# Decoder step on one core: the causal mask of the stick-breaking logits moves from a TensorE product to a GpSimd select

## The chip, the cores and the metric

One NeuronCore of a Trainium2 chip runs the whole program. The metric is the device time of one execution in microseconds (us); where several executions are shown, their median counts. Engines are named as in the profile: PE is TensorE (PEld its weight loads), DVE VectorE, ACT ScalarE, POOL GpSimd, SP the queue that issues the transfers. S, Z, O, TR, OU and three G are the eight PSUM banks.

## The reference, cut to what matters

One layer of a decoder: input projections of 520 token columns (512 prompt tokens and 8 decoding ones), three token mixers, a gated merge, an output projection and an MLP. The change touches the stick-breaking attention of the prompt, 8 heads by 4 blocks of 128 queries. Its logits are strictly causal, a key counts for a query only if it stands before it:

```python
def sb_block(q, k, v, q_pos, k_pos, b_sb):
    z = (jnp.einsum('bqhd,bkhd->bhqk', q, k).astype(jnp.float32) * (HEAD_DIM ** -0.5)
         + b_sb.astype(jnp.float32)[None, :, None, None])
    valid = k_pos[None, :] < q_pos[:, None]
    log_keep = jnp.where(valid, jax.nn.log_sigmoid(-z), 0.0)
    after = lax.cumsum(log_keep, axis=3, reverse=True) - log_keep
    a = jnp.where(valid, jnp.exp(jax.nn.log_sigmoid(z) + after), 0.0)
    return jnp.einsum('bhqk,bkhd->bqhd', a.astype(v.dtype), v)
```

Where a logit is -1e30, both the log of what is kept and the weight come out as 0, so that the mask can be written into the logits.

## The kernel before, in words

All weights are split into a high and a low part so that PE can work with full precision: `split_hi` on ACT (L675, 128x1024) copies the raw tile into whi, `split_lo` (on POOL for nearly all units, L638) subtracts it and writes wlo. A unit is one 128-wide weight tile; a tick is one half (260 columns) of one unit: 24 products G<-xh,whi / xl,whi / xh,wlo in `project` (L1277), in two parts. The result goes to one of three G banks, from which ACT takes it (`take`, L703).

The rest of the kernel is hung between these ticks. `make_plan` (L180) gives every stage a tick; each engine walks through all ticks in order and issues its share of the stages behind its own work of that tick. The order is fixed when the program is written, and each engine works strictly in it.

The 36 steps of the stick-breaking attention, `PSEQ` (L172), are 32 prompt steps "p" (block i of queries, head h, with 128*(i+1) keys) and 4 decoding steps "d". Step m starts at tick 20+m:

- tick 20+m: PE forms the logits in bank S (`p_scores`, L1343): a product of skT and sqT (64 rows, fp32, two records in the profile), and onto its last 128 columns a second, bf16 product of an identity and a strictly upper mask of -1e30 (identb, maskb).
- tick 21+m: ACT (`p_weights`, L779) scales bank S into pz (L786), which frees the bank, then runs Abs, Exp and Ln over it (psp, L796 to L798); DVE (`p_weights`, L1121) makes psp, a scan into pw, and pw minus pz.
- tick 23+m: ACT takes Exp of pw (`p_exp`, L800) at the tick's start; PE turns pw into bank TR (`p_turn`, L1352) at its end; DVE copies it to pT (L1133).
- tick 24+m: PE forms the weighted sum (`p_sum`, L1360) in bank OU.

At every odd tick of this stretch ACT issues a `split_hi` between its take and its `p_weights`, and POOL answers with a `split_lo` of some 2.4 us. POOL has nothing else to do there but one memset. The masks are made once at the program's start:

```python
            nc.gpsimd.affine_select(out=maskb[:], in_=maskb[:], compare_op=ALU.is_gt, fill=MASK, base=0,
                                    pattern=[[-1, P]], channel_multiplier=1).then_inc(consts_made, 1)
```

The chain of one step crosses the engines like this in ACT's part:

```python
                    nc.scalar.activation(z, src[:, keys], ACT.Identity, scale=SCALE,
                                         bias=bsb[:, h:h + 1]).then_inc(of(read, "p_scores", n), 1)
                    await_taken(act, "p_scores", n)
```

Of the kernel before, what the change touches and what calls it, by code (L numbers as in the profile page):

```python
# [10 lines left out]
BF16 = mybir.dt.bfloat16  # L11
I32 = mybir.dt.int32
ALU = mybir.AluOpType
# [3 lines left out]
P = 128  # L17
# [7 lines left out]
SBH = 8  # L25
# [7 lines left out]
MASK = -1e30  # L33
# [77 lines left out]
def at(kind, tile, half=1):  # L111
    return AT[kind, tile, half]
# [59 lines left out]
PSEQ = []  # L172
# [126 lines left out]
def decoder_step(nc, x, o):  # L299

    ctx = ExitStack()
    with ctx:
        def sem(name):
            return ctx.enter_context(nc.semaphore(name))
# [4 lines left out]
        base = 16512  # L309

        def place(name, shape, col, dt=F32):
            return nc.alloc_sbuf_tensor_at(name, shape, dt, offset=base + 4 * col)
# [4 lines left out]
        whi = place("whi", [P, 2, KC, P], 11392, F32R)  # L317
        wlo = place("wlo", [P, 2, KC, P], 13440, F32R)
        ident = place("ident", [P, P], 15488)
        identb = place("identb", [P, P], 15616, BF16)  # L320
        maskb = place("maskb", [P, P], 15680, BF16)
        ones = place("ones", [P, P], 15744)
        cvec = place("cvec", [P, NCV], 15872)
        c0 = 15872 + (NCV + 7) // 8 * 8
# [30 lines left out]
        sqT = place("sqT", [P, 4, TOK], R)  # L355
        skT = place("skT", [P, 4, TOK], R + 2080)
        svT = place("svT", [P, 4, TOK], R + 4160)
        sv_tok = place("sv_tok", [P, QB, 512], R + 7280)
        pz = place("pz", [P, 2, 512], R + 9360)
# [65 lines left out]
        written = {n: sem(f"written_{n}") for n in ("S", "TR", "OU")}  # L425
        read = {n: sem(f"read_{n}") for n in ("S", "TR", "OU", "Z", "O")}
        act_done, dve_done, pool_done = sem("act_done"), sem("dve_done"), sem("pool_done")
        consts_made = sem("consts_made")
# [3 lines left out]
        kv_in = [sem(f"kv_in{i}") for i in range(KVS)]  # L432
        kv_used = sem("kv_used")
        qz_zero, qd_zero_made, qz_made, qd_made = sem("qz_zero"), sem("qd_zero_made"), sem("qz_made"), sem("qd_made")
        p_lnmade, p_wmade, p_amade = sem("p_lnmade"), sem("p_wmade"), sem("p_amade")
        bias_in_slot = [sem(f"bias_in_slot{i}") for i in range(2)]
        l_made, l_pmade = sem("l_made"), sem("l_pmade")
        sk_out, sv_out, dk_out, dv_out, conv_out, conv_copy = (
# [16 lines left out]
        def raw(u):  # L455

            if u < U_MLP:
                return wraw[:, u % WR], w_in_slot[u % WR], 16 * (u // WR + 1)
            m = u - U_MLP
            return mraw[:, m % MR], m_in_slot[m % MR], 16 * (m // MR + 1)  # L460

        def high(u):
            return mhigh[:, u - U_END] if u >= U_END else whi[:, u % 2]

        def low(u):
            return mlow[:, (u - U_MLP) % MR] if u >= U_END else wlo[:, u % 2]
# [12 lines left out]
        def open_bank(pe, *key):  # L479
            name, n = SPOT[key]  # L480
            if n:
                pe.wait_ge(read[name], n)
            return bank[name]

        def await_bank(eng, *key):
            name, n = SPOT[key]
            eng.wait_ge(written[name], n + 1)
            return bank[name]

        def await_taken(eng, *key):  # L490
            name, n = SPOT[key]
            eng.wait_ge(read[name], n + 1)

        def of(sems, *key):
            return sems[SPOT[key][0]]
# [10 lines left out]
        def head(h):  # L506
            return h // 2, slice(HD * (h % 2), HD * (h % 2) + HD)
# [114 lines left out]
        @block.gpsimd  # L622
        def _(pool):
            nc.gpsimd.memset(ones[:], 1.0).then_inc(consts_made, 1)
            nc.gpsimd.memset(ident[:], 0.0).then_inc(pool_done, 1)
            nc.gpsimd.memset(identb[:], 0.0).then_inc(pool_done, 1)
            nc.gpsimd.memset(maskb[:], 0.0).then_inc(pool_done, 1)
            nc.gpsimd.memset(qz[:], 0.0).then_inc(qz_zero, 1)
            nc.gpsimd.memset(Q192[:], 0.0).then_inc(qz_zero, 1)
            nc.gpsimd.memset(wT[:, PAGES * 64:], 0.0).then_inc(qz_zero, 1)  # L630
            pool.wait_ge(pool_done, 3)
            for m in (ident, identb):
                nc.gpsimd.affine_select(out=m[:], in_=m[:], compare_op=ALU.not_equal, fill=1.0, base=0,
                                        pattern=[[-1, P]], channel_multiplier=1).then_inc(consts_made, 1)
            nc.gpsimd.affine_select(out=maskb[:], in_=maskb[:], compare_op=ALU.is_gt, fill=MASK, base=0,
                                    pattern=[[-1, P]], channel_multiplier=1).then_inc(consts_made, 1)

            def split_lo(u):  # L638
                pool.wait_ge(w_hi, u + 1)
                nc.gpsimd.tensor_tensor(low(u), raw(u)[0], high(u).bitcast(F32), ALU.subtract).then_inc(w_lo, 1)  # L640

            split_lo(0)
            for kc in range(1, KC, 2):
                pool.wait_ge(rstd0_made, 2)
                if kc >= 3:
                    pool.wait_ge(xl_made, kc - 1)
                nc.gpsimd.tensor_tensor(xn[:, 1, :], xraw[:, kc, :], rstd0[:], ALU.mult).then_inc(xn_pool, 1)
            split_lo(1)

            def qd_zero(_):  # L650
                pool.wait_ge(xl_made, KC)
                nc.gpsimd.memset(qd[:], 0.0).then_inc(qd_zero_made, 1)

            stages = dict(qd_zero=qd_zero)
            for k, (u, job, h, last) in enumerate(TICKS):
                for v in SPLIT_AFTER.get(k, []):
                    if not LO[v][0]:
                        split_lo(v)
                for stage, n in PLAN[2 * k] + PLAN[2 * k + 1]:
                    if stage in stages:  # L660
                        stages[stage](n)

        @block.scalar
        def _(act):
            done = [0]

            def link(ins):
                done[0] += 1
                ins.then_inc(act_done, 1)
                act.wait_ge(act_done, done[0])  # L670
# [108 lines left out]
            def p_weights(m):  # L779
                what, n = PSEQ[m]  # L780
                if what == "p":
                    i, h = n // SBH, n % SBH
                    keys = slice(0, P * (i + 1))
                    src = await_bank(act, "p_scores", n)
                    z, l = pz[:, m % 2, keys], psp[:, m % 2, keys]
                    nc.scalar.activation(z, src[:, keys], ACT.Identity, scale=SCALE,  # L786
                                         bias=bsb[:, h:h + 1]).then_inc(of(read, "p_scores", n), 1)
                    await_taken(act, "p_scores", n)
                else:
                    act.wait_ge(kv_used, 8 * (n + 1))  # L790
                    src = bank[SPOT["d", n][0]]
                    z, l = pz[:, m % 2, :], psp[:, m % 2, :]
                    nc.scalar.activation(z, src[:, :], ACT.Identity, scale=SCALE,
                                         bias=bcol).then_inc(of(read, "d", n), 1)
                    await_taken(act, "d", n)
                link(nc.scalar.activation(l, z, ACT.Abs))  # L796
                link(nc.scalar.activation(l, l, ACT.Exp, scale=-1.0))
                nc.scalar.activation(l, l, ACT.Ln, bias=1.0).then_inc(p_lnmade, 1)  # L798
# [78 lines left out]
            def h_ready_tile(t):  # L877
                act.wait_ge(dve_took, EVAC[at("out", t)][1])
                if t:
# [5 lines left out]
            stages = dict(qz=qz_fill, qd=qd_fill, sv_rows=sv_rows, dv_rows=dv_rows, dvs=dvs_fill, p_weights=p_weights,  # L885
                          p_exp=p_exp, p_turn=p_turn, p_sum=p_sum, v_red=v_red, l_weights=l_weights,
                          l_turn=l_turn, l_out=l_out, s_soft=s_soft, s_turn=s_turn, s_red=s_red,
                          branch_split=branch_split)
# [375 lines left out]
        def _(pe):  # L1264
            def mm(out, lhsT, rhs, start, stop, **kw):
                return nc.tensor.matmul(out, lhsT, rhs, start=start, stop=stop, **kw)  # L1266
# [1 line left out]
            def turn(out, in_, rows=P):  # L1268
                return nc.tensor.transpose(out, in_, ident[0:rows, 0:rows])  # L1269

            pe.wait_ge(consts_made, 4)
            pe.wait_ge(xacc_made, KC)
            for h in range(2):
                dst = open_bank(pe, "x_var", h)
# [68 lines left out]
            def p_scores(n):  # L1343
                i, (t, rows) = n // SBH, head(n % SBH)
                keys = P * (i + 1)
                if n == 0:
                    pe.wait_ge(act_took, EVAC[at("sk", 3)][1])
                dst = open_bank(pe, "p_scores", n)
                mm(dst[:, 0:keys], sqT[rows, t, P * i:P * i + P], skT[rows, t, 0:keys], True, False)
                mm(dst[:, keys - P:keys], identb[:], maskb[:], False, True).then_inc(of(written, "p_scores", n), 1)  # L1350

            def p_turn(m):  # L1352
                what, n = PSEQ[m]
# [143 lines left out]
            def l_out(t):  # L1497
# [4 lines left out]
            stages = dict(sv_rows=sv_rows, dv_rows=dv_rows, dk=dk, p_scores=p_scores, p_turn=p_turn, p_sum=p_sum,  # L1502
                          v_sum=v_sum, v_red=v_red, s_k=s_k, s_self=s_self, s_turn=s_turn, s_v=s_v,
                          s_vself=s_vself, s_red=s_red, l_scores=l_scores, l_turn=l_turn, l_sum=l_sum, l_out=l_out)
# [160 lines left out]
```

## Time and profile before

| | before |
|---|---|
| median of 3 executions | 1193.66 us (1190.55 to 1194.98) |
| the profiled execution, its own time | 1195.64 us |
| its span | 1193.9 us |
| mean granted clock of PE | 0.982 of full speed |
| busy: PE, PEld, DVE, ACT, POOL | 94%, 83%, 34%, 37%, 27% |
| the stick-breaking steps of the prompt | ticks 20 to 60, from 106 to 349 us |

A row of the order in time reads: start in us, duration in us, engine, source line, operation, what is written and read, shape, how many are merged, and in brackets how long the engine was idle before it and who ended that. "MATMUL S<-maskb,identb" is the mask product, "pz<-S" the copy out of bank S, "TR<-ident,pw" the turn of the weights.

### The profile page before, as it was taken

The numbers are of one execution on the slowest core, as the hardware profiler recorded it, in microseconds if no ns is written. First come the engines' busy times: TensorE is split into PE (matmuls) and PEld (weight loads), VectorE is DVE, ScalarE is ACT, GpSimd is POOL, SyncE is SP. The second block draws the span as 40 slices with busy tenths as digits, with TensorE's granted clock in tenths as the row PEclk, the third lists the DMA queues.
The fourth block names the chain that finished last, engine by engine and source line by source line (L and its number), as shares of the span: only waits on it lengthen the run. The fifth ranks groups of instructions, "written<-read, shape, count | busy, mean of one in ns | idle before, by whom it ended". The sixth has DMA issues, their size and how long they took to land.

```text
span 1193.9 us, 21778 instructions
## 1 busy us (share of the span) xinstructions
PE 1119.1 (94%) x8650; PEld 994.3 (83%) x8650; DVE 406.0 (34%) x680; ACT 442.0 (37%) x796; POOL 318.0 (27%) x146
## 2 busy tenths in 40 slices
PE   2998899999999999999999999998999999999995
PEld 1886666667776767667899999998999999999995
DVE  6101233443432244241204344675312312222444
ACT  5223354555442322324332232345413413413544
POOL 3432122211112111100121212123444444444540
PEclk9999899999999999999999999998999999999998
DMA  7369666655468645544124223472765674665402
GB/s 234 124 196 307 223 204 195 184 209 181 142 210 295 193 156 185 150 151 147 54 89 161 89 97 98 159 295 78 270 218 180 238 263 172 236 244 206 159 1 72
DMA packets 65847, 210.91 MB, mean 177 GB/s; under 512 B 7850, under 2 KB 10059, under 8 KB 63571
## 3 DMA queue, kind: packets, MB, share of 16 engines
q1 hardware_dynamic: 65746, 209.52, 52.3%
q8 instruction: 69, 1.13, 0.4%
q14 instruction: 32, 0.25, 0.1%
HBM read 202.02 MB, written 51.48 MB: 212 GB/s over the span
## 4 chain that ended last, share of the span: by engine, by line
PE 86%; ACT 5%; DVE 4%; issue 2%; DMA 1%; SPq 0%; POOL 0%; DVEq 0%; ACTq 0%; POOLq 0%
PE G L1266 54%; PE S L1266 10%; PE Z L1266 9%; PE O L1266 8%; PE OU L1266 3%; PE TR L1269 2%; ACT whi L673 2%; DVE convy L960 1%; ACT pz L786 1%; DVE xl L960 1%; DMA wraw<-in_w_in_dram 1%; DMA xraw<-in_xt_dram 0%; PE TR L1266 0%; DVE mtmp L960 0%; DVE macc L957 0%
## 5 line engine op out<-in xcount | busy, mean ns | idle before, releaser
L1266 PE MATMUL G<-xh,whi 128*128 128x260 f32 x1312 | 389.5, 297 | 13.5 <-DVE xl L960 11.8
L1266 PE MATMUL G<-xl,whi 128*128 128x260 f32 x1312 | 376.6, 287 | 0.0
L1266 PE MATMUL G<-xh,wlo 128*128 128x260 f32 x1312 | 376.1, 287 | 0.0
L640 POOL TENSOR_TENSOR wlo<-wraw,whi 128x1024 fp32r<-128x1024 f32 x63 | 153.4, 2435 | 618.4 <-ACT whi L673 618.4
L1266 PEld LDWEIGHTS G<-xh,whi 128*128 128x128 f32 x1312 | 253.0, 193 | 52.6 <-issue 37.9
L1266 PEld LDWEIGHTS G<-xl,whi 128*128 128x128 f32 x1312 | 253.6, 193 | 0.0
L1266 PEld LDWEIGHTS G<-xh,wlo 128*128 128x128 f32 x1312 | 253.4, 193 | 0.0
L640 POOL TENSOR_TENSOR wlo<-mraw,whi 128x1024 fp32r<-128x1024 f32 x56 | 134.9, 2409 | 200.6 <-ACT whi L673 200.5
L673 ACT ACTIVATE whi<-wraw 128x1024 fp32r<-128x1024 f32 x84 | 88.4, 1053 | 85.6 <-PE G L1266 77.2
L673 ACT ACTIVATE whi<-mraw 128x1024 fp32r<-128x1024 f32 x56 | 59.4, 1061 | 157.0 <-PE G L1266 54.6
L960 DVE SCALAR_TENSOR_TENSOR psp<-pz,psp 128x512 f32<-128x512 f32 (+3 forms) x36 | 24.6, 684 | 142.2 <-ACT psp L798 142.2
L960 DVE SCALAR_TENSOR_TENSOR lg<-S,bias 128x256 f32<-128x256 f32 (+3 forms) x48 | 22.0, 457 | 105.2 <-PE S L1266 105.2
L731 ACT ACTIVATE tg<-G,cvec 128x260 f32<-128x260 f32 x48 | 22.9, 477 | 88.7 <-PE G L1266 88.7
L957 DVE TENSOR_TENSOR wlo<-wraw,whi 128x1024 fp32r<-128x1024 f32 x21 | 25.7, 1224 | 86.6 <-ACT whi L673 86.6
L673 ACT ACTIVATE lT<-TR 128x256 f32<-128x256 f32 (+3 forms) x48 | 19.6, 409 | 94.4 <-PE TR L1269 94.4
L1266 PE MATMUL G<-hidl,whi 128*128 128x260 f32 x192 | 54.4, 283 | 0.0
L1266 PE MATMUL G<-hidh,whi 128*128 128x260 f32 x192 | 54.3, 283 | 0.0
L1266 PE MATMUL G<-hidh,wlo 128*128 128x260 f32 x192 | 54.1, 282 | 0.0
L957 DVE TENSOR_TENSOR hidl<-msq,hidh 128x260 fp32r<-128x260 f32 x64 | 45.6, 714 | 4.8 <-ACT hidh L673 4.8
L1266 PE MATMUL G<-binh,whi 128*128 128x260 f32 x160 | 45.5, 284 | 1.6 <-issue 1.6
L1266 PEld LDWEIGHTS OU<-dv_tok,lT 128*128 128x128 f32 x216 | 28.0, 190 | 22.1 <-issue 17.4
L957 DVE TENSOR_TENSOR hT<-hT,G 128x260 f32<-128x260 f32 x47 | 19.9, 423 | 77.0 <-PE G L1266 77.0
(270 smaller groups left out, 2246.1 us busy)
## 6 DMA issues: line engine op xcount, KB each, us to landing
wraw<-in_w_in_dram SPq DMA_DIRECT2D x66, 512.0 KB, 4.8
kv<-in_kpool_dram SPq DMA_DIRECT2D x128, 256.0 KB, 3.2
kv<-in_vpool_dram SPq DMA_DIRECT2D x128, 256.0 KB, 3.1
mraw<-in_w_up_dram SPq DMA_DIRECT2D x32, 512.0 KB, 3.4
mraw<-in_w_down_dram SPq DMA_DIRECT2D x32, 512.0 KB, 3.4
out_win_k_kept_dram<-in_cache_win_k_dram SPq DMA_DIRECT2D x8, 2047.0 KB, 9.5
out_win_v_kept_dram<-in_cache_win_v_dram SPq DMA_DIRECT2D x8, 2047.0 KB, 10.8
wraw<-in_w_ab_dram SPq DMA_DIRECT2D x8, 512.0 KB, 3.3
```

The lines of the kernel that those rows point to most:

```text
L640: nc.gpsimd.tensor_tensor(low(u), raw(u)[0], high(u).bitcast(F32), ALU.subtract).then_inc(w_lo, 1)
L673: return nc.scalar.activation(out, in_, ACT.Copy, **kw)
L731: nc.scalar.activation(tg[tile % 4][:, g, half(h)], src, ACT.Tanh, scale=0.5, bias=bgate[:, g, tile:tile + 1]).then_inc(act_took, 1)
L786: nc.scalar.activation(z, src[:, keys], ACT.Identity, scale=SCALE, bias=bsb[:, h:h + 1]).then_inc(of(read, "p_scores", n), 1)
L957: return nc.vector.tensor_tensor(out, a, b, op)
L960: return nc.vector.scalar_tensor_tensor(out, a, scalar, b, op0, op1)
L1266: return nc.tensor.matmul(out, lhsT, rhs, start=start, stop=stop, **kw)
L1269: return nc.tensor.transpose(out, in_, ident[0:rows, 0:rows])
```

## The change

The mask is no longer added by PE. POOL writes it: behind ACT's copy of the logits into pz, a select on POOL fills the part on and above the diagonal of pz's last 128 columns with -1e30, in place, and counts the new semaphore `p_masked`. ACT, which read pz back at once, now waits for `p_masked` before Abs. The 32 mask products and the two bf16 constants with their memsets and selects go away, and PE's first wait is for two constants in place of four.

```diff
@@ the constants on POOL
-            nc.gpsimd.memset(identb[:], 0.0).then_inc(pool_done, 1)
-            nc.gpsimd.memset(maskb[:], 0.0).then_inc(pool_done, 1)
...
-            pool.wait_ge(pool_done, 3)
-            for m in (ident, identb):
-                nc.gpsimd.affine_select(out=m[:], in_=m[:], compare_op=ALU.not_equal, fill=1.0, base=0,
-                                        pattern=[[-1, P]], channel_multiplier=1).then_inc(consts_made, 1)
-            nc.gpsimd.affine_select(out=maskb[:], in_=maskb[:], compare_op=ALU.is_gt, fill=MASK, base=0,
+            pool.wait_ge(pool_done, 1)
+            nc.gpsimd.affine_select(out=ident[:], in_=ident[:], compare_op=ALU.not_equal, fill=1.0, base=0,
                                     pattern=[[-1, P]], channel_multiplier=1).then_inc(consts_made, 1)
@@ a new stage on POOL
-            stages = dict(qd_zero=qd_zero)
+            def p_weights(m):
+                what, n = PSEQ[m]
+                if what == "p":
+                    i = n // SBH
+                    await_taken(pool, "p_scores", n)
+                    own = pz[:, m % 2, P * i:P * i + P]
+                    nc.gpsimd.affine_select(out=own, in_=own, compare_op=ALU.is_gt, fill=MASK, base=0,
+                                            pattern=[[-1, P]], channel_multiplier=1).then_inc(p_masked, 1)
+
+            stages = dict(qd_zero=qd_zero, p_weights=p_weights)
@@ p_weights on ACT
-                    await_taken(act, "p_scores", n)
+                    act.wait_ge(p_masked, n + 1)
@@ the start of PE
-            pe.wait_ge(consts_made, 4)
+            pe.wait_ge(consts_made, 2)
@@ p_scores on PE
-                mm(dst[:, 0:keys], sqT[rows, t, P * i:P * i + P], skT[rows, t, 0:keys], True, False)
-                mm(dst[:, keys - P:keys], identb[:], maskb[:], False, True).then_inc(of(written, "p_scores", n), 1)
+                mm(dst[:, 0:keys], sqT[rows, t, P * i:P * i + P], skT[rows, t, 0:keys], True,
+                   True).then_inc(of(written, "p_scores", n), 1)
```

POOL's order before, from the last load of the start-up to the end of the weight splits that read wraw; wlo is the low part of a weight tile and waits for ACT's high part (w_hi):

```order
L640 TENSOR_TENSOR wlo<-wraw,whi 128x1024 [waits w_hi] x19
L652 MEMSET qd 128x1536 [waits xl_made]
L640 TENSOR_TENSOR wlo<-wraw,whi 128x1024 [waits w_hi] x43
```

POOL's order now, the first part of the same stretch:

```order
L633 TENSOR_TENSOR wlo<-wraw,whi 128x1024 [waits w_hi] x12
L653 AFFINE_SELECT pz<-pz 128x128 [waits read_S]
L633 TENSOR_TENSOR wlo<-wraw,whi 128x1024 [waits w_hi]
L653 AFFINE_SELECT pz<-pz 128x128 [waits read_S] x2
L633 TENSOR_TENSOR wlo<-wraw,whi 128x1024 [waits w_hi]
L653 AFFINE_SELECT pz<-pz 128x128 [waits read_S] x2
L633 TENSOR_TENSOR wlo<-wraw,whi 128x1024 [waits w_hi]
L653 AFFINE_SELECT pz<-pz 128x128 [waits read_S]
L633 TENSOR_TENSOR wlo<-wraw,whi 128x1024 [waits w_hi]
```

The selects stand one or two to a gap between the splits: the select of an odd tick comes directly behind that tick's split, the one of an even tick has no split ahead of it.

ACT's order around tick 27, before (whi is the high part of the tile that POOL's split reads):

```order
L673 ACTIVATE dqT<-G 128x260 [waits made]
L673 ACTIVATE whi<-wraw 128x1024 [waits made,w_in_slot0]
L786 ACTIVATE pz<-S,cvec 128x128 [waits written_S]
L796 ACTIVATE psp<-pz 128x128 [waits read_S]
L797 ACTIVATE psp<-psp 128x128 [waits act_done]
L798 ACTIVATE psp<-psp 128x128 [waits act_done]
L804 ACTIVATE pw<-pw 128x128 [waits p_wmade]
```

And now:

```order
L675 ACTIVATE dqT<-G 128x260 [waits made]
L675 ACTIVATE whi<-wraw 128x1024 [waits made,w_in_slot0]
L788 ACTIVATE pz<-S,cvec 128x128 [waits written_S]
L798 ACTIVATE psp<-pz 128x128 [waits p_masked]
L799 ACTIVATE psp<-psp 128x128 [waits act_done]
L800 ACTIVATE psp<-psp 128x128 [waits act_done]
L806 ACTIVATE pw<-pw 128x128 [waits p_wmade]
```

Nothing moved on ACT; one instruction waits for POOL instead of for ACT itself, and the Exp of pw, which belongs to an earlier step, stands behind it.

## Rows read from the trace of the kernel before

**Rows 1.** The page: the span and PE's busy time.

```profile
span 1193.9 us, 21778 instructions
PE 1119.1 (94%) x8650; PEld 994.3 (83%) x8650; DVE 406.0 (34%) x680; ACT 442.0 (37%) x796; POOL 318.0 (27%) x146
```

**Rows 2.** The page: the chain that ended last, by engine.

```profile
PE 86%; ACT 5%; DVE 4%; issue 2%; DMA 1%; SPq 0%; POOL 0%; DVEq 0%; ACTq 0%; POOLq 0%
```

**Rows 3.** Waits of PE, 104 to 350 us: in total, times, longest (us).

```profile
PE S L1266 <- ACT pz L786: 19.0, 17, 4.5
```

**Rows 4.** Order in time, PE: a prompt step with 256 keys, mask product included.

```profile
171.22 0.70 PE L1266 MATMUL S<-skT,sqT 64*128 64x256 f32 x2 [1.68 <-ACT pz L786]
...
171.85 0.23 PE L1266 MATMUL S<-maskb,identb 128*128 128x128 bf16 x1
...
172.09 0.28 PE L1266 MATMUL G<-xl,whi 128*128 128x260 f32 x1
```

**Rows 5.** Order in time, PE: logits of the other attention, same shape, no mask.

```profile
386.27 0.70 PE L1266 MATMUL S<-dkT,dqT 64*128 64x256 f32 x2
...
386.90 0.39 PE L1266 MATMUL G<-xh,whi 128*128 128x260 f32 x1
...
387.12 0.28 PE L1266 MATMUL G<-xl,whi 128*128 128x260 f32 x1
```

**Rows 6.** Groups by form on POOL: busy us, mean ns of one, idle before.

```profile
L640 POOL TENSOR_TENSOR wlo<-wraw,whi 128x1024 fp32r<-128x1024 f32 x63 | 153.4, 2435 | 618.4 <-ACT whi L673 618.4
L633 POOL TENSOR_SCALAR_AFFINE_SELECT ident<-ident 128x128 f32<-128x128 f32 x1 | 0.3, 292 | 0.0
```

**Rows 7.** Order in time, ticks 27 and 28.

```profile
151.63 2.39 POOL L640 TENSOR_TENSOR wlo<-wraw,whi 128x1024 fp32r<-128x1024 f32 x1 [10.23 <-ACT whi L673]
...
151.84 0.31 ACT L796 ACTIVATE psp<-pz 128x128 f32<-128x128 f32 x1
...
152.75 0.29 ACT L804 ACTIVATE pw<-pw 128x128 f32<-128x128 f32 x1
...
152.87 1.30 DVE L960 SCALAR_TENSOR_TENSOR psp<-pz,psp 128x128 f32<-128x128 f32 x1 [1.74 <-ACT psp L798]
...
153.97 0.33 PE L1269 MATMUL TR<-ident,pw 128*128 128x128 f32 x1
```

**Rows 8.** Order in time, ticks 37 and 38.

```profile
209.32 2.40 POOL L640 TENSOR_TENSOR wlo<-wraw,whi 128x1024 fp32r<-128x1024 f32 x1 [8.37 <-ACT whi L673]
...
209.63 0.42 ACT L796 ACTIVATE psp<-pz 128x256 f32<-128x256 f32 x1
...
210.85 0.40 ACT L804 ACTIVATE pw<-pw 128x256 f32<-128x256 f32 x1
...
212.20 0.44 PE L1269 MATMUL TR<-ident,pw 128*128 128x128 f32 x2
```

**Rows 9.** Order in time, ticks 47 and 48.

```profile
269.95 2.41 POOL L640 TENSOR_TENSOR wlo<-wraw,whi 128x1024 fp32r<-128x1024 f32 x1 [10.57 <-ACT whi L673]
...
270.38 0.53 ACT L796 ACTIVATE psp<-pz 128x384 f32<-128x384 f32 x1
...
273.46 0.52 ACT L804 ACTIVATE pw<-pw 128x384 f32<-128x384 f32 x1
...
274.04 0.55 PE L1269 MATMUL TR<-ident,pw 128*128 128x128 f32 x3 [0.58 <-ACT pw L804]
```

**Rows 10.** Order in time, ticks 39 and 40.

```profile
221.39 0.61 ACT L804 ACTIVATE pw<-pw 128x512 f32<-128x512 f32 x1
...
224.70 0.66 PE L1269 MATMUL TR<-ident,pw 128*128 128x128 f32 x4
```

**Rows 11.** Stretches behind waits: us, busy by engine (instructions), granted clock, DMA share, GB/s.

```profile
171.00:177.00 6.00, 5.78 (x43) 3.73 (x43) 2.11 (x3) 1.62 (x5) 2.26 (x1) 1.00 0.42 148
184.00:190.00 6.00, 6.00 (x35) 4.71 (x39) 1.60 (x3) 2.17 (x6) 1.49 (x1) 0.72 0.63 192
...
582.00:588.00 6.00, 6.00 (x38) 6.00 (x39) 0.00 (x0) 0.66 (x2) 0.00 (x0) 0.72 0.29 87
```

More of the change, by code:

```diff
@@ L319, in decoder_step @@
         ident = place("ident", [P, P], 15488)
-        identb = place("identb", [P, P], 15616, BF16)
-        maskb = place("maskb", [P, P], 15680, BF16)
         ones = place("ones", [P, P], 15744)
@@ L434, in decoder_step @@
         qz_zero, qd_zero_made, qz_made, qd_made = sem("qz_zero"), sem("qd_zero_made"), sem("qz_made"), sem("qd_made")
-        p_lnmade, p_wmade, p_amade = sem("p_lnmade"), sem("p_wmade"), sem("p_amade")
+        p_lnmade, p_wmade, p_amade, p_masked = sem("p_lnmade"), sem("p_wmade"), sem("p_amade"), sem("p_masked")
         bias_in_slot = [sem(f"bias_in_slot{i}") for i in range(2)]
```

## The prediction, made before the changed kernel ran

> **What bounds the kernel now.** I read the page first: PE works 94% of the span [rows 1], and of the chain that ended last 86% lie on it [rows 2]. So only what lengthens or shortens PE's own row moves the end. Then the waits of PE in the stretch of the change: it idles there nearly only for bank S, freed by ACT's copy into pz, 17 times and 19.0 us in all, 4.5 us of them in one wait [rows 3]. All three engines that the change touches meet in that stretch, and what must be seen is the order in time around each step.
>
> **What the change takes from PE.** The mask product shows 0.23 us [rows 4], and 32 of them would be 7.4 us. But matmuls are pipelined, so I compare what a step costs with and without it. With 256 keys and the mask, the second G product begins 172.09 - 171.22 = 0.87 us after the logits' start [rows 4]. The other attention forms logits of the same shape with no mask, and there it is 387.12 - 386.27 = 0.85 us [rows 5]. The mask runs in the bubble that the change from S to G leaves anyway. It gives back 0.02 us, and 32 times that is **0.6 us**.
>
> A rule speaks for a larger gain. The Trainium skill, TensorE: Matmul & The Clock Gate, section "Back-to-back issue gap", gives about 81 ns for a sustained pair of weight load and product with 128 columns. By it 32 products would be 2.6 us and the sum below 6.4 us instead of 8.4. The trace's pair of steps disagrees, and I go by it.
>
> **What the change adds on POOL.** A select of 128x128 fp32 took 0.292 us at the start of the program; a weight split takes 2.435 us for 1024 columns [rows 6], which is 0.30 us for 128, so the two agree. That is the value I take; bounds are below. 32 selects are 9.3 us on an engine that is busy 27% [rows 1], free in itself. What counts is where they stand. ACT now copies, waits for POOL, then goes on to Abs, Exp, Ln and, behind them, to the Exp of pw for which PE's next turn waits.
>
> *Even ticks* (15 steps "p"): POOL is idle. ACT stands still for 0.29 us and two hand-overs. A hand-over between engines takes 0.06 us where the rows show one at its limit: pw ends at 273.98 and PE's turn starts at 274.04 [rows 9]. About 0.4 us each, and ACT is busy only 37% [rows 1]: nothing of it reaches PE.
>
> *Odd ticks* (17 steps "p"): `split_hi` stands right before the copy on ACT, and so POOL has just begun the split of 2.4 us when the copy is done. The select waits for all of it. In tick 27 POOL's split ends at 151.63 + 2.39 = 154.02, the select at 154.31, ACT can go on at about 154.38 instead of 151.84 [rows 7]. That is a **delay of 2.5 us**, and of 2.4 to 2.5 us in ticks 37 and 47 [rows 8, 9]. It is paid where PE's turn (TR<-ident,pw) of the next tick stands less than that behind the end of pw's Exp:
>
> - tick 28: pw ends at 152.75 + 0.29 = 153.04 and PE turns at 153.97, 0.93 us later [rows 7]. 2.54 - 0.93 and 0.06 to hand over: **1.7 us** of new wait.
> - tick 38: split ends 211.72, select 212.01, Abs 212.08 instead of 209.63, delay 2.45; pw ended 211.25, the turn stood at 212.20, 0.95 later [rows 8]: **1.5 us**, 1.6 with the hand-over.
> - tick 48: PE already waits 0.58 us for pw there, so there is no cover. Split ends 272.36, Abs 272.72 instead of 270.38 [rows 9]: **2.3 us** on top, a wait of 2.9 us.
>
> In both of the first two PE has no decoding product between its G products, so the tick is short. I put each of the other odd ticks to the same test: the narrowest is tick 40, where pw ends at 222.00 and the turn stands at 224.70, 2.7 us of cover against 2.5 [rows 10]. ACT's next take is up to 2 us late after some of them, but its G bank is wanted three ticks later. The splits themselves do not get later: POOL's next one waits for ACT two ticks on. Together **5.6 us**.
>
> *DVE* is not late by all of that. Its psp<-pz,psp of 128 columns lasted 1.30 us in tick 27 and ended at 154.17, right behind POOL's split at 154.02 [rows 7]: it stood still while POOL worked. The Trainium skill, SBUF — State Buffer, section "Who interferes with whom", says that a DVE instruction with two SBUF inputs and a GpSimd one that reads SBUF lock each other out for a whole instruction; the trace agrees. In the changed kernel DVE starts after the select and is no longer held, so its chain is late by about 1.5 us, not 2.5, and pw of that step is needed more than a tick later. Nothing for PE.
>
> *The start*: PE waits for DVE there, not for the constants. Nothing. No transfer is moved; those that wait for PE come later by as much as PE does.
>
> **What the waits do to PE's clock.** Behind some waits the granted clock falls from 2.4 to 1.2 GHz for a while: the 6 us from 184 on, behind such a wait, show 0.72, while behind the wait of 1.68 us that ends at 171.22 [rows 4] they show 1.00 [rows 11]. A fall costs 6 x 0.28 = 1.7 us. From the wait at 171.22 to the stretch at 582, I find nine waits of over 1.1 us, and five had a fall behind them; first and last of those stretches, and one more, stand in [rows 11]. The two longest of the nine both had one, of the seven from 1.1 to 1.7 us three. For new waits of 1.7, 1.6 and 2.9 us that makes 0.43 + 0.43 + 1, about two falls: **3.4 us**.
>
> **The sum.** 5.6 - 0.6 + 3.4 = **8.4 us**. Against the profiled execution's own 1195.64 that is 1204.0; it stood 2.0 above the median of 1193.66, and against that the forecast is **1202.0 us**, slower by 0.7%. What can be told from no change is about 0.5%, 6 us.
>
> **The rivals.**
>
> *The clock doesn't follow* (no new fall, or one that takes an old one's place, or some of the three waits better covered than here). Then it is 5.6 - 0.6 = 5.0, 1198.7 us, not to be told from no change. For it: four of the seven waits of this size had no fall. Against it: the one of 2.9 us.
>
> *The select is dearer on pz than on the constant.* Only one size and one place was seen; a far bound is a whole microsecond, below half a split [rows 6]. Then 0.7 us more at each of three places is 2.1, tick 40 is short of cover by 0.5, and its like (cover of 2.7 to 3 us) by a few tenths each: some 3.6 in all, 1205.7 us. For it: the agreement with the split's price per column says nothing of a fixed part in another state. Against it: 0.292 includes the fixed part.
>
> *PE gets the whole product back* (the other side). If removing it freed 0.23 us each time, in place of 0.02, PE would gain 7.4 and lose 5.6: 1191.9 us, and with two falls 1195.3, in either case no longer slower. It decides from 5.6 / 32 = 0.175 us a product. Against it stands the pair of steps [rows 4, 5], 0.87 and 0.85 us; for it only that the two steps follow different work.
>
> That the select doesn't do what it should, I see no way for: ACT's own wait for it comes ahead of every reader of pz.
>
> **How the numbers follow.** Forecast, three waits and one to three falls (6.7 to 10.1): 0.58. Clock doesn't follow: 0.27. Dearer select: 0.10. Whole product back, or the three places covered: 0.05. The bound of 6 us lies just under the case of one fall, so 0.62 for slower by over 0.5%, taken from the forecast's case and the dearer select with a little off; 0.34 within 0.5%; 0.04 faster. The range goes from 1196.5, half of the waits and no fall, to 1207.0, three falls and a select of twice the price; it leaves out some 0.15.
>
> **What would show it right or wrong.** In the profile after: PE's waits in the turn (TR<-ident,pw) for pw, 0.6 us before in one wait [rows 9], should be about 6 us in three, the longest 2.9 and in tick 48; a new wait of ACT's psp for POOL's pz of some 2.4 us at 17 steps and 0.4 at 15, 47 us in all or a little less; psp<-pz,psp on DVE without the long cases; bank S steps of 0.85 us; 32 selects of 0.29 us. If the turn's waits make less than 3 us, my cover is wrong; if they are there and the time isn't, it is the clock; if the step without mask is far below 0.85, it is the price of the product.

## The result and the profile after

The changed kernel takes 1205.06 us in the median of six executions (1200.87 to 1209.96), against 1193.79 us of the kernel before: a ratio of 1.010, with a 95% interval of 1.0072 to 1.0128. Six more executions in a later comparison gave 1204.75 us and 1.008 (1.0054 to 1.0106). The forecast was 1202.0 us with a range of 1196.5 to 1207.0, so the change makes the kernel slower, as forecast, and by some more than forecast. Times of kernels are medians of executions, and each kernel is compared with executions of the kernel before that ran beside it.

The page of the changed kernel, its span and busy time; its own time is 1203.70 us, 8.1 more than that of the profiled execution before:

```profile
span 1201.9 us, 21772 instructions
...
PE 1121.4 (93%) x8618; PEld 995.2 (83%) x8618; DVE 399.9 (33%) x680; ACT 441.0 (37%) x796; POOL 325.9 (27%) x174
```

PE is busy 2.3 us longer than before [rows 1] although 32 products are gone; its products run longer where the clock is lower. The rest of the 8.0 us by which the span grew, 5.7 us, is idle time of PE. The chain by engine is nearly what it was [rows 2], with POOL at 1% where it had 0%:

```profile
PE 86%; ACT 5%; DVE 4%; issue 3%; DMA 1%; POOL 1%; SPq 1%; DVEq 0%; ACTq 0%; POOLq 0%
```

The waits of PE from 104 to 360 us; the numbers are the total, how many and the longest, in us:

```profile
PE S L1268 <- ACT pz L788: 19.1, 17, 4.6
PE TR L1271 <- ACT pw L806: 5.7, 3, 2.8
```

The waits for bank S are as long as before [rows 3]. New is the wait of PE's turn for ACT's pw: three waits and 5.7 us, where before there was one of 0.6 us. They stand in ticks 28, 38 and 48 and last 1.51, 1.38 and 2.83 us. What ACT waits for in the same stretch:

```profile
ACT psp L798 <- POOL pz L653: 45.4, 32, 2.5
```

At 17 odd ticks it waits 1.9 to 2.5 us, at 15 even ones mostly 0.47. The select itself, as a group (busy us, mean ns, idle before), takes 307 ns in the mean, against 292 on a constant [rows 6]:

```profile
L653 POOL TENSOR_SCALAR_AFFINE_SELECT pz<-pz 128x128 f32<-128x128 f32 x32 | 9.8, 307 | 61.0 <-ACT pz L788 61.0
```

Ticks 27 and 28 of the changed kernel in order of time, the answer to [rows 7]:

```profile
148.93 2.39 POOL L633 TENSOR_TENSOR wlo<-wraw,whi 128x1024 fp32r<-128x1024 f32 x1 [6.69 <-ACT whi L675]
...
151.27 0.29 POOL L653 TENSOR_SCALAR_AFFINE_SELECT pz<-pz 128x128 f32<-128x128 f32 x1
151.60 0.31 ACT L798 ACTIVATE psp<-pz 128x128 f32<-128x128 f32 x1 [2.50 <-POOL pz L653]
...
152.50 0.29 ACT L806 ACTIVATE pw<-pw 128x128 f32<-128x128 f32 x1
152.62 0.29 DVE L962 SCALAR_TENSOR_TENSOR psp<-pz,psp 128x128 f32<-128x128 f32 x1 [4.20 <-ACT psp L800]
...
152.84 0.33 PE L1271 MATMUL TR<-ident,pw 128*128 128x128 f32 x1 [1.51 <-ACT pw L806]
```

The split runs from 148.93 to 151.32, the select directly behind it. ACT goes on at 151.60 after standing still for 2.50 us, the Exp of pw ends at 152.79, and PE turns 0.05 us later, having waited 1.51. Ticks 37 and 38, the answer to [rows 8]:

```profile
209.62 2.38 POOL L633 TENSOR_TENSOR wlo<-wraw,whi 128x1024 fp32r<-128x1024 f32 x1 [6.72 <-ACT whi L675]
...
212.28 0.42 ACT L798 ACTIVATE psp<-pz 128x256 f32<-128x256 f32 x1 [2.38 <-POOL pz L653]
...
213.95 0.44 PE L1271 MATMUL TR<-ident,pw 128*128 128x128 f32 x2 [1.38 <-ACT pw L806]
```

Ticks 47 and 48, the answer to [rows 9]:

```profile
273.15 2.40 POOL L633 TENSOR_TENSOR wlo<-wraw,whi 128x1024 fp32r<-128x1024 f32 x1 [6.95 <-ACT whi L675]
...
275.50 0.29 POOL L653 TENSOR_SCALAR_AFFINE_SELECT pz<-pz 128x128 f32<-128x128 f32 x1
275.83 0.52 ACT L798 ACTIVATE psp<-pz 128x384 f32<-128x384 f32 x1 [2.29 <-POOL pz L653]
...
278.91 0.52 ACT L806 ACTIVATE pw<-pw 128x384 f32<-128x384 f32 x1
...
279.48 0.55 PE L1271 MATMUL TR<-ident,pw 128*128 128x128 f32 x3 [2.83 <-ACT pw L806]
```

Here the wait grew from 0.58 to 2.83 us, by 2.25. The clock behind the three waits (stretch, its length, busy by engine, granted clock, DMA share, GB/s):

```profile
153.00:159.00 6.00, 6.00 (x38) 5.05 (x40) 3.69 (x7) 3.52 (x8) 0.00 (x0) 0.72 0.78 244
214.00:220.00 6.00, 6.00 (x32) 2.94 (x32) 4.33 (x8) 2.95 (x6) 0.00 (x0) 0.72 0.30 112
280.00:286.00 6.00, 6.00 (x33) 4.82 (x33) 3.38 (x5) 2.58 (x5) 0.00 (x0) 0.72 0.01 2
```

All three show 0.72 as the mean granted clock: in each the clock fell from 2.4 to 1.2 GHz for a while. A step with 256 keys, for [rows 4, 5]:

```profile
171.58 0.70 PE L1268 MATMUL S<-skT,sqT 64*128 64x256 f32 x2 [1.68 <-ACT pz L788]
...
172.20 0.39 PE L1268 MATMUL G<-xh,whi 128*128 128x260 f32 x1
...
172.43 0.29 PE L1268 MATMUL G<-xl,whi 128*128 128x260 f32 x1
```

From the logits to the second G product it takes 172.43 - 171.58 = 0.85 us, what the maskless step of the other attention took [rows 5], and 0.02 less than with the mask [rows 4].

**The time split in two.** Each execution comes with its span and its mean granted clock. Span times (1 - clock) is the time that the clock withheld; the remainder is an estimate of what the span would be at full clock, good as far as PE sets the pace. Every execution's time is 1.7 to 1.9 us longer than its span. The clock is given to three decimals, which fixes one execution's split to 0.6 us only, so I use means over executions. The ratio is to the kernel before in the same comparison:

| kernel | executions | median us | ratio to before (95%) | withheld us | remainder us |
|---|---|---|---|---|---|
| before, all | 73 | 1195.15 | 1 | 20.2 | 1173.2 |
| changed, all | 12 | 1204.76 | 1.010 and 1.008 | 25.5 | 1177.5 |
| select first, all ticks | 12 | 1193.68 | 0.9983 (0.9968 to 0.9998) | 17.9 | 1173.6 |
| select first, three ticks | 12 | 1193.84 | 0.9991 (0.9977 to 1.0005) | 19.3 | 1172.8 |
| before, no mask product | 12 | 1194.84 | 0.9998 (0.9981 to 1.0015) | 19.6 | 1172.9 |
| changed, waits filled | 10 | 1200.55 | 1.0053 (1.0032 to 1.0074) | 21.6 | 1177.7 |
| before, wait only | 6 | 1206.11 | 1.0095 (1.0062 to 1.0127) | 27.5 | 1177.5 |
| changed, select twice | 4 | 1207.24 | 1.0097 (1.0066 to 1.0128) | 27.4 | 1177.9 |
| before, copy first | 6 | 1183.13 | 0.9892 (0.9865 to 0.9918) | 17.1 | 1164.0 |
| select first, copy first | 6 | 1185.71 | 0.9909 (0.9882 to 0.9935) | 19.1 | 1164.3 |

The change costs 1177.5 - 1173.2 = 4.3 us of remainder and 25.5 - 20.2 = 5.3 us withheld. With the spread of the executions (95%) the first is known to 0.9 us and the second to 2.0.

### The profile page after: what moved, and what is told of

Same layout as the page of the kernel before. It is cut to its first block, busy times and chain, and to the rows that moved or that the text cites. A ratio compares the mean times of both kernels' runs of the same rounds, so it can differ in the third digit from the quotient of the medians.

```text
span 1201.9 us, 21772 instructions
## 1 busy us (share of the span) xinstructions
PE 1121.4 (93%) x8618; PEld 995.2 (83%) x8618; DVE 399.9 (33%) x680; ACT 441.0 (37%) x796; POOL 325.9 (27%) x174
## 4 chain that ended last, share of the span: by engine, by line
PE 86%; ACT 5%; DVE 4%; issue 3%; DMA 1%; POOL 1%; SPq 1%; DVEq 0%; ACTq 0%; POOLq 0%
PE G L1268 54%; PE S L1268 10%; PE Z L1268 8%; PE O L1268 8%; PE OU L1268 3%; PE TR L1271 2%; ACT whi L675 2%; DVE convy L962 1%; ACT pz L788 1%; DVE xl L962 1%; DMA wraw<-in_w_in_dram 0%; PE TR L1268 0%; DMA xraw<-in_xt_dram 0%; DVE mtmp L962 0%; DVE macc L959 0%
## 5 line engine op out<-in xcount | busy, mean ns | idle before, releaser
L962 DVE SCALAR_TENSOR_TENSOR psp<-pz,psp 128x512 f32<-128x512 f32 (+3 forms) x36 | 18.5, 513 | 177.3 <-ACT psp L800 177.3
L675 ACT ACTIVATE lT<-TR 128x256 f32<-128x256 f32 (+3 forms) x48 | 19.6, 409 | 97.3 <-PE TR L1271 97.3
L1268 PE MATMUL G<-binh,whi 128*128 128x260 f32 x160 | 45.4, 284 | 1.6 <-issue 1.6
```

What stands on the lines that cost most here:

```text
L675: return nc.scalar.activation(out, in_, ACT.Copy, **kw)
L962: return nc.vector.scalar_tensor_tensor(out, a, scalar, b, op0, op1)
```

## The experiments

**The kernel before, again.** No edit.

> The kernel before once more, unchanged, for its own spread, the clock of each of its executions and as a second profile. Every theory: 1191 to 1196 us, three or four waits of PE fewer than in the changed kernel, and about 20 to 23 us of span times missing clock (the changed kernel's six executions show 21.6 to 30.2 by the same product). If the clock's falls make part of the loss, these products stand lower here than there by 2 to 5 us; if only the waits do, they stand the same.

1195.12 us, ratio 1.0005 (0.9988 to 1.0023); withheld 15.5 to 22.8 us, 19.7 in the mean, so the two kernels differ in this part too. The changed kernel again:

> The changed kernel once more, unchanged, for more executions beside the next two. Split by the clock: span times missing clock was 27.1 us in the median of its first six executions against 20.3 of the kernel before, and the rest of the span 1177.0 against 1172.8. If the loss is waits of some 4 to 5 us and clock of some 6 to 7 us, both come again here: 26 to 28 and 1176 to 1178, and 1203 to 1206 us.

1204.75 us, as expected. Withheld is 24.5 us in the mean of these six, the remainder 1178.0. The remainder came again as said. The withheld part was below the 26 to 28 expected: six executions (21.6 to 29.0) don't fix it to better than some 2 us, which is why the table takes all twelve. Its profile has 5.7 us in three waits once more, with falls of the clock that begin at about 153.5 and 279.8 us, behind the first and third. The one in the middle had none. A fall came at 228.6 instead, directly behind a wait of 1.15 us for bank S that ends at 227.10; the kernel before has this wait too (1.15 us, it ends at 226.51), without a fall.

**Select first, all ticks.** On POOL only the order changes:

```diff
-                for v in SPLIT_AFTER.get(k, []):
-                    if not LO[v][0]:
-                        split_lo(v)
+                first = 21 <= k <= 56
+                if not first:
+                    for v in SPLIT_AFTER.get(k, []):
+                        if not LO[v][0]:
+                            split_lo(v)
                 for stage, n in PLAN[2 * k] + PLAN[2 * k + 1]:
                     if stage in stages:
                         stages[stage](n)
+                if first:
+                    for v in SPLIT_AFTER.get(k, []):
+                        if not LO[v][0]:
+                            split_lo(v)
```

> The changed kernel with one thing turned round on POOL: in ticks 21 to 56 the select goes ahead of the weight split of the same tick. Theory A (the loss is the select's place behind the split): ACT waits 0.4 to 0.5 us for POOL at each of 32 steps, 14 to 16 us in all in place of 45; PE's turns wait for pw only in tick 48, 0.6 to 1.1 us; the time goes back to that of the kernel before within 3 us, 1192 to 1196. Theory B (a select costs more than its own row, wherever it stands): at least half of the 11 us stays, 1199 or more. Theory C (the split on POOL comes late and PE waits for wlo): new waits of PE for wlo.

1193.68 us: all of the loss is gone, and the interval of the ratio, 0.9968 to 0.9998, even ends just below 1. The waits of PE and of ACT from 104 to 360 us:

```profile
PE S L1274 <- ACT pz L794: 19.7, 17, 5.2
...
PE TR L1277 <- ACT pw L812: 1.0, 1, 1.0
```

```profile
ACT psp L804 <- POOL pz L653: 15.4, 32, 0.8
```

ACT's wait is 0.47 us at 31 of 32 steps, 15.4 us in all as against 45.4. PE keeps one wait of 1.0 us for pw, in tick 48, and has none for wlo. Theories B and C fall: what the select costs PE is its place.

**Select first in ticks 27, 37 and 47 alone.** The same edit with `first = k in (27, 37, 47)`.

> The changed kernel with the select ahead of the split in ticks 27, 37 and 47 alone; in the other fourteen odd ticks it stays behind. Theory A (three places without cover pay all of it): PE's waits for pw fall from 5.7 us in three to about 1 us in one, ACT still waits some 38 us for POOL, and the time is that of the kernel before within 3 us, 1192 to 1197. Theory D (the many covered delays of 2.4 us cost something too, by late takes or a late DVE): the time stays well above, 1199 or more.

```profile
PE S L1274 <- ACT pz L794: 17.6, 17, 3.1
...
PE TR L1277 <- ACT pw L812: 1.0, 1, 1.0
```

```profile
ACT psp L804 <- POOL pz L653: 39.8, 32, 2.7
```

1193.84 us, as fast as with all ticks turned round. ACT still waits 39.8 us for POOL, only 5.6 us less than in the changed kernel, and that is enough. The 14 other delays of 1.9 to 2.7 us cost nothing that can be measured. Theory D falls, and the three places named ahead are the whole loss.

**The product's price.** The kernel before, with the mask product left out and nothing in its place, so that the logits are not masked:

```diff
-                mm(dst[:, 0:keys], sqT[rows, t, P * i:P * i + P], skT[rows, t, 0:keys], True, False)
-                mm(dst[:, keys - P:keys], identb[:], maskb[:], False, True).then_inc(of(written, "p_scores", n), 1)
+                mm(dst[:, 0:keys], sqT[rows, t, P * i:P * i + P], skT[rows, t, 0:keys], True,
+                   True).then_inc(of(written, "p_scores", n), 1)
```

> The kernel before with the 32 mask products on PE left out and nothing in their place, so the logits aren't masked; all else stays. It measures what the product costs PE. Rows of the two attentions: 0.02 us each, 0.6 us in all, 1193 us or no difference that can be measured, and a step with 256 keys of 0.85 us from the logits to the second G product. The Trainium skill's sustained 81 ns a pair (TensorE: Matmul & The Clock Gate): 2.6 us, 1191 us and 0.79. The product's whole row of 0.23 us: 7.4 us, 1186 us and 0.64.

```profile
166.88 0.70 PE L1266 MATMUL S<-skT,sqT 64*128 64x256 f32 x2 [1.68 <-ACT pz L786]
...
167.51 0.39 PE L1266 MATMUL G<-xh,whi 128*128 128x260 f32 x1
...
167.73 0.29 PE L1266 MATMUL G<-xl,whi 128*128 128x260 f32 x1
```

0.9998 (0.9981 to 1.0015), and 167.73 - 166.88 = 0.85 us a step. The interval reaches to 2.3 us of gain, so the time alone speaks clearly against 7.4 us. The Trainium skill, TensorE: Matmul & The Clock Gate, section "Back-to-back issue gap", gives about 81 ns for a sustained pair, from which 2.6 us and a step of 0.79 us were estimated; the time only just speaks against that, and the step's own rows, 0.85 us, disagree with it.

**The wait without the select.** The kernel before keeps its mask product and has no select; ACT only waits at the odd ticks until POOL's split is done:

```diff
                     await_taken(act, "p_scores", n)
+                    for v in SPLIT_AFTER.get(21 + m, []):
+                        act.wait_ge(*split(v))
```

> The kernel before, with its mask product on PE and no select, and one wait added: in the odd ticks ACT waits after its copy into pz until POOL's split of that tick is done. If only the place behind the split counts, this has nearly the whole loss: a delay shorter by the select and its hand-over (2.1 in place of 2.5 us), so waits of PE for pw of 1.2, 1.1 and 2.5 us, 4.8 us in all against 5.7, and 1200 to 1204 us. If the select, its memory traffic or the lost product make a good part of it, 1198 or less.

```profile
PE TR L1271 <- ACT pw L806: 5.1, 3, 2.6
```

```profile
ACT psp L798 <- POOL wlo L640: 34.6, 17, 2.3
```

1206.11 us, above the 1200 to 1204 expected: the whole loss, and not less than the changed kernel's. The remainder is that of the changed kernel too, 1177.5 us, known to 1.0 us. Neither the select, nor its traffic, nor the missing product has a part in the loss that can be measured. PE's waits are 5.1 us where 4.8 were expected.

**The select done twice.** Each step's select is followed by a second one in place that waits for the first.

> The changed kernel with the select done twice at every step (the second changes nothing), so 0.3 to 0.35 us more in ACT's wait each time. If delay is paid only at the three places, PE's waits for pw grow by 0.3 to 0.35 us each, to 6.7 us, and the time by 1 to 2 us. If the other odd ticks have little cover left (tick 40 has 0.2 us by the rows of the kernel before), more places wait: four or more, 7.5 us, and 3 us or more on the time with the clock's part.

```profile
PE TR L1275 <- ACT pw L810: 7.0, 3, 3.3
```

Still three waits, each longer by 0.43 us on average (7.0 - 5.7 = 1.3), where 0.3 to 0.35 were expected. 1207.24 us is 2.5 above the changed kernel's 1204.76, more than the 1 to 2 expected, and the remainder moved by 0.4 us where 1.3 was to be seen: four executions are too few to settle the size. That no fourth place waits for pw, the profile shows.

**The waits filled.** In the changed kernel PE forms products that nobody uses while it waits:

```diff
+                if m in (5, 15, 25):
+                    k = 23 + m
+                    pe.wait_ge(*took(PREV[k + 1]))
+                    for r in range({5: 12, 15: 11, 25: 23}[m]):
+                        mm(bank[BANK[k + 1]][:, 0:HALF], high(TICKS[k][0])[:, r % KC, :], xh[:, r % KC, half(1)],
+                           True, True)
                 pe.wait_ge(p_amade, m + 1)
```

> The changed kernel with 12, 11 and 23 products ahead of PE's turn in ticks 28, 38 and 48, as long as the three waits there (0.12 us each), into a G bank that the next tick overwrites. They compute nothing that is used; they keep PE at work while it waits for pw. Theory A (the clock falls because PE idles in these three places): the missing clock goes from 27 back to 20 to 22 us, the rest stays at 1177, 1198 to 1199 us in all. Theory B (the falls have another cause, such as the later phase of the whole stretch): missing clock stays at 26 to 28, and the time at 1203 to 1206 or above.

Tick 28 in order of time, with the twelve products and the turn ahead of which PE no longer waits, and then the three stretches behind:

```profile
152.17 1.70 PE L1268 MATMUL G<-xh,whi 128*128 128x260 f32 x12
...
153.75 0.33 PE L1271 MATMUL TR<-ident,pw 128*128 128x128 f32 x1
```

```profile
152.00:158.00 6.00, 6.00 (x49) 5.07 (x51) 2.61 (x6) 4.50 (x12) 0.46 (x2) 1.00 0.77 226
213.00:219.00 6.00, 6.00 (x46) 3.85 (x46) 4.58 (x8) 3.21 (x7) 0.00 (x0) 1.00 0.30 115
276.00:284.00 8.00, 8.00 (x61) 6.64 (x59) 4.66 (x7) 4.25 (x13) 0.00 (x0) 1.00 0.23 96
```

The granted clock is 1.00 in all three, where the changed kernel had 0.72. Withheld falls from 25.5 to 21.6 us, against 20.2 of the kernel before, the remainder stays (1177.7), and the time is 1200.55 us, 4.2 less, though PE does 46 products more. So most of the withheld part comes from PE standing still in these three places: 3.9 of 5.3 us, a difference that these executions fix to 2.9 us. That it is more than nothing is clear; that it is nearly all of the 5.3 is not. Withheld and remainder are as expected; the time lies above the 1198 to 1199 expected because these left out the 1.8 us between span and time.

**ACT's copy ahead of its split.** The profiles suggest one thing beside the change: PE waits for bank S because ACT runs `split_hi` (1.05 us) before the copy that frees the bank. The kernel before, with this turned round in the odd ticks 25 to 55 and, as its condition also lets through, for the decoding step of tick 21:

```diff
+                early = [e for e in PLAN[2 * k + 1] if e[0] == "p_weights" and k % 2 and k != 23]
+                for stage, n in early:
+                    p_weights(n)
                 for v in SPLIT_AFTER.get(k, []):
                     split_hi(v)
...
                 for stage, n in PLAN[2 * k + 1]:
-                    if stage in stages:
+                    if stage in stages and (stage, n) not in early:
                         stages[stage](n)
```

> The kernel before, mask product and all, with ACT's order turned round in the odd ticks 25 to 55: its p_weights (copy into pz, Abs, Exp, Ln) goes ahead of split_hi, which takes 1.05 us. Bank S is then free some 0.95 us sooner in these ticks. Theory A (PE's waits for S are ACT's order): of the 18 to 19 us of PE's waits for S some 6 to 7 go, with perhaps one fall of the clock, and the time is 1186 to 1189. Theory B (the S wait in odd ticks is bound by something behind ACT, or the later split makes PE wait for wlo): no difference or slower.

```profile
PE S L1269 <- ACT pz L786: 9.0, 8, 2.4
```

1183.13 us, 1.1% faster than the kernel before and below the 1186 to 1189 expected. PE's waits for S go from 17 to 8 and from 19.0 us [rows 3] to 9.0, where 6 to 7 us less were expected; 2.1 of these 10 us are the wait in tick 22, 2.4 in place of 4.5 us, and would belong to the decoding step moved in tick 21, which no run tests by itself (in a second profile of the kernel before this wait is 3.6). Withheld is 3 us lower too, but six executions fix that to some 4 us only. One thing shows in tick 31 that had not been counted, on DVE:

```profile
168.77 0.47 ACT L786 ACTIVATE pz<-S,cvec 128x256 f32<-128x256 f32 x1
...
169.29 0.70 PE L1269 MATMUL S<-skT,sqT 64*128 64x256 f32 x2 [0.73 <-ACT pz L786]
...
170.49 1.05 ACT L673 ACTIVATE whi<-wraw 128x1024 fp32r<-128x1024 f32 x1
...
171.62 2.38 POOL L640 TENSOR_TENSOR wlo<-wraw,whi 128x1024 fp32r<-128x1024 f32 x1 [9.56 <-ACT whi L673]
171.80 2.47 DVE L960 TENSOR_TENSOR pw<-pw,pz 128x256 f32<-128x256 f32 x1
```

pw<-pw,pz of 256 columns takes 2.47 us instead of some 0.43. It started 0.18 us behind POOL's split, which runs from 171.62 to 174.00, and ended 0.27 us behind it. It costs PE nothing: PE's waits for pw stay at one of 0.6 us.

With the select in place of the product, select ahead of split and the same turn on ACT:

> The same turn on ACT, with the mask by POOL's select and the select ahead of the split on POOL. Theory A: PE's waits for S as in the one with the product, a wait of about 1 us for pw in tick 48, and the time within 2 us of it, 1186 to 1190. Theory B (the chain that the select makes longer by 0.5 us a step costs more where ACT has less slack): 1190 or more.

1185.71 us, ratio 0.9909 (0.9882 to 0.9935). The interval overlaps with that of the product's version (0.9865 to 0.9918); the remainders are 1164.3 and 1164.0. PE's waits for S are 9.8 us in 8, and for pw there is one of 1.0 us, as expected. Both beat the two kernels of this case, and which way of masking is better can't be told from them.

## Why the prediction was right, and where it was off

- *The product's price*, "it gives back 0.02 us": right, by the step's rows (0.85 us) and by the kernel without it, which is no faster within 0.2%.
- *The even ticks*, "about 0.4 us each", "nothing of it reaches PE": 0.47 us, and none of PE's waits for pw follows such a delay; the three follow the odd ticks 27, 37 and 47.
- *The delay at the odd ticks*, 2.5 us in tick 27 and 2.4 to 2.5 in 37 and 47: ACT waits 2.50, 2.38 and 2.29 us there, and as little as 1.9 where another copy stands between `split_hi` and the copy into pz.
- *Where it is paid*: three places, all three named, no fourth. Turning the order round there alone brings everything back.
- *How much is paid there*, "5.6 us": from the start of POOL's split to the turn it takes 3.91, 4.33 and 6.33 us, against 2.34, 2.88 and 4.09 before [rows 7 to 9], so the turns are later by 1.57, 1.45 and 2.24 us, 5.3 in all. The forecast was 0.3 above because each delay was taken some 0.09 us too long: the select starts 0.05 us before the split's row ends, and ACT goes on 0.04 us behind the select, not 0.07. The waits in the profile make a little less, 1.51 + 1.38 + 2.25 = 5.1, since the turns of ticks 28 and 38 used to start 0.07 us before the product ahead of them ended. With the 0.6 us of the products that leaves 4.7; the remainder moved by 4.3, and the forecast's terms make 5.0. All three agree within the spread.
- *The clock*, "about two falls: 3.4 us": this term was mis-sized. The withheld time grew by 5.3 us, three falls of 1.7 and not two. In the four profiles with the three waits (the changed kernel twice, the wait alone and the select twice) the first and third wait had a fall behind them every time, and the second twice; where it had none, a fall came behind the wait of 1.15 us for S, some 16 us later. For the first two waits that is six falls of eight, where the forecast took three of seven from earlier waits; seven were too small a base. The stretch from 100 to 370 us agrees: the six profiles without these three waits at their length (before twice, no mask product, select first twice, waits filled) withhold 8.5, 5.1, 3.4, 5.1, 3.4 and 5.1 us there, 5.1 in the mean; the four with them 8.5, 8.5, 11.9 and 11.9, 10.2 in the mean. How a single fall comes about stays open: the wait of 1.26 us for S that ends at 295.21 before has one behind it in both profiles of the kernel before, and in one of these four.
- *The sum*, 8.4 us: 9.6 us between all executions of both. The clock's term was 1.9 short, and the rest 0.7 too high, which hides a part of it. The forecast of 1202.0 was 3 us low against the first comparison's 1205.06. Of that 1.2 is the sum; 1.5 is the base, since the three executions it started from had a median of 1193.66 and all 73 have 1195.15; the rest is the spread of the changed kernel's own.
- *The range*: its ends are not what their terms add up to. Half of the waits and no fall make 1193.66 + 2.8 - 0.6 = 1195.9, where 1196.5 stands. Three falls and a select of twice the price make 1193.66 + 5.6 - 0.6 + 5.1 and some 1.1 for the select, 1204.9, where 1207.0 stands. The measured 1205.06 lies within the range as stated, and just beyond the end that its terms give, so that part of the hit is luck; with the difference of 9.6 from all executions it would be 1203.3, inside both.
- *The rivals*: "the clock doesn't follow" is out, for the withheld time grew by 5.3 us and the filled waits give 3.9 of it back; "the select is dearer on pz" is out, at 0.307 us in the mean; "PE gets the whole product back" is out by the kernel without the product.
- *DVE*: psp<-pz,psp went from a mean of 684 ns, the first row, to 513, the second:

```profile
L960 DVE SCALAR_TENSOR_TENSOR psp<-pz,psp 128x512 f32<-128x512 f32 (+3 forms) x36 | 24.6, 684 | 142.2 <-ACT psp L798 142.2
L962 DVE SCALAR_TENSOR_TENSOR psp<-pz,psp 128x512 f32<-128x512 f32 (+3 forms) x36 | 18.5, 513 | 177.3 <-ACT psp L800 177.3
```

The long cases are gone, as said: the longest is 0.69 us now, the 128-column one of tick 27 0.29 in place of 1.30 [rows 7], and it now starts behind POOL's work.

## What to carry to other kernels

When work is handed to another engine, the price of waiting for it is what stands in that engine's queue, and not only the operation itself. Look at what stands there directly ahead of it, here 2.4 us of weight split ahead of 0.29 us of select, and put the short work that others wait for first. Whether such a delay costs anything is read where its last consumer is: of 17 delays of about the same length three were paid, in the two short ticks and in the one where PE waited already. Before an operation on the engine that bounds the kernel is taken away, measure a step with it against one without it: a product with a row of 0.23 us was worth 0.02. And look for the same order in the other queues: ACT's copy ahead of its split was worth 1.1%.

## What the runs showed of the hardware that was not expected

- The idle time of PE in these three places costs about twice its length: 4.3 us of new remainder came with 5.3 us of withheld clock, and filling the waits with useless products made the kernel 4.2 us faster. It is no fixed factor: ACT's copy ahead of its split took 9.2 us off the remainder and about 3 off the withheld time.
- The spread between executions of one kernel is to a good part the clock's: over 73 executions of the kernel before, the withheld time runs from 14.3 to 25.2 us, with a standard deviation of 2.6 us against 1.6 for the remainder.
- A DVE operation with both operands in SBUF that starts just behind POOL's split lasts until the split is done: 2.47 us for one of 0.43, in every odd tick with 256 keys of the kernel that copies first, where the row of the kernel before had shown 1.30 us [rows 7]. The Trainium skill, SBUF — State Buffer, section "Who interferes with whom", says that a DVE instruction with two SBUF inputs contends with a GpSimd instruction that reads SBUF, and the trace agrees.
